# A float32r gather for two experts at a time, weights in runs of 8 KB, and one wait less in a mixture-of-experts layer

## The reference

```python
h2 = rms_norm(x, g_norm_ffn) * (1 + scale2) + shift2          # scale2, shift2: columns of c_act @ w_ada
p_group = softmax(h2 @ w_rg + b_rg);  g_sel = argmax            # 4 groups
logits_sel = (h2 @ w_re + b_re)[group g_sel]                    # 8 experts in the group
pi_top, e_in = top_k(softmax(logits_sel), 2)                    # 2 experts for each token
weights = pg_top * pi_top / sum(pi_top)
for e in range(32):                                             # the tokens that chose e
    h = silu(xc @ w_g[e]) * (xc @ w_u[e])                       # w_g, w_u: 1024 x 512
    y = (h @ w_d[e]) * weight                                   # w_d: 512 x 1024
x = x + gate2 * sum of a token's two y
```

## Time and profile before

| | |
|---|---|
| median of 3 runs | 1013.75 us |
| the profiled execution: its time | 1013.75 us |
| its span in the trace | 1011.9 us |
| TensorE (PE) busy | 924.4 us (91%) |
| VectorE (DVE) busy | 468.7 us (46%) |
| ScalarE (ACT) busy | 193.4 us (19%) |
| GpSimd (POOL) busy | 125.2 us (12%) |
| DMA | 271.01 MB, mean 268 GB/s |
| chain that ended last | DMA 41%, PE 41%, SP's queue 6%, DVE 5% |

### The profile page before, as it was taken

The page is one execution under the profiler, slowest core; times in us unless marked ns, Lnnn a source line. Parts: engine busy times, 40 slices in busy tenths (PEclk is TensorE's granted clock), DMA queues, the critical chain, the costliest instruction groups (busy, mean ns, idle before and its releaser), DMA issues.

```text
span 1011.9 us, 11514 instructions
## 1 busy us (share of the span) xinstructions
PE 924.4 (91%) x4335; PEld 497.7 (49%) x4335; DVE 468.7 (46%) x762; ACT 193.4 (19%) x327; POOL 125.2 (12%) x159
## 2 busy tenths in 40 slices
PE   3699999988989999699899999999999999999980
PEld 2266789977776665388433333333333333333330
DVE  2432555367687666523643343343343343343334
ACT  3432333333335332202100000000000000000000
POOL 1000222004223122600000000000000000000000
PEclk9799999998999999799999999999999999999996
DMA  9886672202050204623799999999999999999976
GB/s 347 289 284 229 220 245 84 84 1 95 22 156 27 84 1 166 248 100 124 281 380 396 392 397 393 395 395 394 397 393 396 392 397 393 395 395 396 396 277 257
DMA packets 116278, 271.01 MB, mean 268 GB/s; under 512 B 8565, under 2 KB 20869, under 8 KB 112661
## 3 DMA queue, kind: packets, MB, share of 16 engines
q1 hardware_dynamic: 112116, 264.41, 70.5%
q0 software_dynamic: 2944, 5.29, 1.5%
q10 hardware_dynamic: 1184, 0.87, 0.3%
HBM read 263.70 MB, written 11.03 MB: 272 GB/s over the span
## 4 chain that ended last, share of the span: by engine, by line
DMA 41%; PE 41%; SPq 6%; DVE 5%; issue 4%; ACT 3%; DVEq 0%; POOLq 0%; POOL 0%; ACTq 0%
DMA arena<-in_w_expert_up 38%; PE ps L639 23%; SPq L407 4%; PE ps L982 3%; PE ps L595 2%; PE ps L791 2%; SPq L362 2%; PE ps L1000 1%; PE ps L959 1%; PE ps L816 1%; DMA arena<-in_w_ada 1%; DMA arena<-y_rows 1%; ACT xn L1173 1%; PE ps L800 1%; PE ps L745 1%
## 5 line engine op out<-in xcount | busy, mean ns | idle before, releaser
L982 PE MATMUL ps<-arena,hT 128*64 128x512 f32 x1024 | 225.7, 592 | 3.5 <-DMA arena<-in_w_expert_up 1.9
L982 PEld LDWEIGHTS ps<-arena,hT 128*64 128x64 f32 x1024 | 73.7, 137 | 149.6 <-issue 145.1
L1000 PE MATMUL ps<-arena,hT 128*64 128x512 f32 x512 | 116.9, 598 | 0.6 <-issue 0.6
L959 PE MATMUL ps<-xn,hT 128*64 128x512 f32 x512 | 115.4, 592 | 0.9 <-DVE hT L1671 0.9
L639 PE MATMUL ps<-slot_r,xs_r 128*128 128x512 f32 x320 | 106.1, 404 | 0.5 <-issue 0.5
L639 PE MATMUL ps<-xs_r,slot_r 128*128 128x512 f32 x320 | 103.7, 406 | 3.0 <-DVE hT_r L1376 2.9
L1795 DVE TENSOR_SCALAR hT<-hT 128x256 f32<-128x256 f32 x32 | 9.4, 294 | 191.4 <-ACT hT L1282 191.4
L639 PE MATMUL ps<-slot_r,hT_r 128*128 128x512 f32 x224 | 88.6, 395 | 0.0
L639 PEld LDWEIGHTS ps<-slot_r,xs_r 128*128 128x128 f32 x320 | 77.1, 261 | 10.6 <-ACT arena L1147 2.5
L1282 ACT ACTIVATE hT<-ps 128x256 f32<-128x256 f32 x32 | 12.3, 384 | 359.2 <-PE ps L982 359.2
L959 PEld LDWEIGHTS ps<-xn,hT 128*64 128x64 f32 x512 | 36.6, 137 | 73.1 <-issue 72.0
(11 more groups left out here) (261 smaller groups left out, 963.5 us busy)
## 6 DMA issues: line engine op xcount, KB each, us to landing
arena<-in_w_expert_gate SPq DMA_DIRECT2D x64, 1024.0 KB, 13.2
arena<-in_w_expert_up SPq DMA_DIRECT2D x64, 1024.0 KB, 14.6
arena<-in_w_expert_down SPq DMA_DIRECT2D x32, 2048.0 KB, 17.0
xn<-in_w_ada SPq DMA_DIRECT2D x16, 1024.0 KB, 5.0
arena<-in_w_in SPq DMA_DIRECT2D x12, 1024.0 KB, 7.8
arena<-in_w_ada SPq DMA_DIRECT2D x8, 1024.0 KB, 14.3
arena<-in_w_branch_gate SPq DMA_DIRECT2D x4, 2048.0 KB, 8.4
xs<-in_x SPq DMA_DIRECT2D x8, 512.0 KB, 8.5
```

The lines of the kernel that those rows point to most:

```text
L959: mm = pe.matmul(ps[64 * h:64 * h + 64, 0, :], hot[:, hb, t, :], xn[:, t, h * CH:(h + 1) * CH], start=(t == 0), stop=(t == NT - 1), skip_g ...
L982: mm = pe.matmul(ps[64 * h:64 * h + 64, 2, :], xeT[:, k % 4, k // 4, :], w_gu(b)[:, :, k, 256 * h:256 * h + 256], start=(k == 0), stop=(k ...
L1000: mm = pe.matmul(ps[64 * h:64 * h + 64, 4, :], hhT[:, f % 2, 64 * (f // 2):64 * (f // 2) + 64], w_dn(b)[:, f, h * CH:(h + 1) * CH], start= ...
```

## The change

- Two experts are gathered with one 0/1 matrix of 128 slots (`hot_r`), in float32r. x1 is kept as two float32r parts, `xs_r` (rounded, by ScalarE) and `xn_r` (the rest, by GpSimd), and each part is multiplied, so a gather of one half of the width is 8 products of 128x512. It is no longer normalised before the gather: `rstd_by_slot` gathers 1/rms of each slot with four small products, VectorE adds the two parts (`keep_rstd`), and ScalarE applies it as it takes the gather from PSUM.
- Partition p holds rows 8p to 8p+7 of each weight (`by_run`), so all expert weights come in runs of 8 KB. x1, the router's weights, the gain and the two columns of scale and shift are laid out to match; the columns go through HBM (`columns` on GpSimd) and no longer through transposes.
- `refill` asks for both halves of gate and up at once.
- transpose_x stands ahead of transpose_h. One buffer of results (`ye`) takes the place of two. x1 as float32 is put together again by VectorE behind expert 30.

```diff
             def load_gu_half(e, b, kh):
-                rows = slice(kh * D // 2, (kh + 1) * D // 2)
...
-                    src = w[0, bass.ds(e, 1), rows].rearrange("e (k p) n -> p (e k) n", p=P)
-                    sp.dma_start(w_gu(b)[:, g, ks], src).then_inc(gu_in[b][kh], 16)
+                    src = w[0, bass.ds(e, 1)].rearrange("e (p k) n -> p (e k n)", k=KC)[:, run]
+                    sp.dma_start(w_gu(b)[:, g, ks].rearrange("p k n -> p (k n)"), src).then_inc(gu_in[b][kh], 16)
...
-            def refill(e, b, last, loads):
+            def refill(e, b):
                 sp.wait_ge(gu_ps, e + 1)
-                load_gu_half(e + NBUF, b, 0)
-                sp.wait_ge(gu_in[last][1], loads * 32)
-                load_gu_half(e + NBUF, b, 1)
+                load_gu(e + NBUF, b)
                 sp.wait_ge(dn_ps, e + 1)
                 load_dn(e + NBUF, b)
...
+            def columns(r):
+                at = 64 * (1 - r)
+                pool.wait_ge(mod_rows, r + 2)
+                pool.dma_start(mod_2[r].rearrange("(j n) -> j n", j=2), modr[at:at + 64:32, :]).then_inc(mod_out, 16)
+                pool.wait_ge(mod_out, 16 * (r + 1))
+                pool.dma_start(cols[:, 3 - r, :], by_run(mod_2[r])).then_inc(cols_in, 16)
...
+            for t in range(NT):
+                pool.wait_ge(hi1_ok, t + 1)
+                pool.wait_ge(x1t_ps, t + 1)
+                pool.tensor_tensor(xn_r[:, t, :], xn[:, t, :], xs_r[:, t, :].bitcast(F32), ALU.subtract
+                                   ).then_inc(lo1_ok, 1)
...
+            def rstd_by_slot(q):
...
                 for t in range(NT):
-                    for h in range(2):
-                        mm = pe.matmul(ps[64 * h:64 * h + 64, 0, :], hot[:, hb, t, :],
-                                       xn[:, t, h * CH:(h + 1) * CH], start=(t == 0), stop=(t == NT - 1),
-                                       skip_group_check=True)
+                    mm = pe.matmul(ps[:, 3, 256:258], hot_r[:, t, :], rstd_r[:, t, :], start=(t == 0),
+                                   stop=(t == NT - 1), skip_group_check=True)
+                mm.then_inc(sr_ps, 1)
+
+            def gather(g, half):
...
+                for t in range(NT):
+                    for part in (xs_r, xn_r):
+                        mm = pe.matmul(ps[:, 6 * half, :], hot_r[:, t, :], part[:, t, half * CH:(half + 1) * CH],
+                                       start=(t == 0 and part is xs_r), stop=(t == NT - 1 and part is xn_r))
...
-            def expert(e, b, hb, loads, more=True):
-                gate_up(e, b, loads)
+            def expert(e, b, loads, xb, j, pair, more=True):
+                gate_up(e, b, loads, xb, j)
                 if not later(e):
                     slot_tables(0)
                 if more:
-                    gather(e + 1, 1 - hb)
+                    if j == 0:
+                        rstd_by_slot(pair + 1)
+                    gather(e + 2, j)
+                    transpose_x(e + 2)
                 else:
                     keep_clock(3)
                 transpose_h(e)
-                if more:
-                    transpose_x(e + 1)
                 down(e, b, loads)
...
-                xt = xs[:, t, j * CH:(j + 1) * CH]
-                dve.tensor_tensor(xt, xt, out_ps, ALU.add).then_inc(x1_ok, 1)
+                xt = xs[:, t, j * CH:(j + 1) * CH].rearrange("p (c k) -> p k c", k=KC)
+                dve.tensor_tensor(xn[:, t, :].rearrange("p (k c) -> p k c", k=KC)[:, :, 64 * j:64 * j + 64], xt,
+                                  out_ps.rearrange("p (c k) -> p k c", k=KC), ALU.add).then_inc(x1_ok, 1)
...
+            for e in range(NE - 4, NE):
+                expert(e, e % 2, e // 2, e // 2 % 2, more=(e < NE - 2))
+                if e == NE - 2:
+                    for t in range(NT):
+                        link(dve.tensor_tensor(x1n[:, t, :].rearrange("p (c k) -> p c k", k=KC),
+                                               xs_r[:, t, :].bitcast(F32).rearrange("p (k c) -> p c k", k=KC),
+                                               xn_r[:, t, :].bitcast(F32).rearrange("p (k c) -> p c k", k=KC),
+                                               ALU.add))
```

More of the change, by code:

```diff
@@ L224, in hybrid_layer @@
                                     for i in range(3))
-        idx = [sb(f"idx{b}", [P, 1], I32) for b in range(2)]
+        idx = sb("idx", [P, 1], I32)
+        rstd_r = sb("rstd_r", [P, NT, 2], F32R)
+        slot_rstd = sb("slot_rstd", [P, 1])
+        x1n = arena[:, EXP_W:EXP_W + NT * D].rearrange("p (t n) -> p t n", t=NT)
         wcol = sb("wcol", [P, 1])
@@ L569, in store @@
                 pool.indirect_dma_start(
[L570 to L578, removed]
+                    out=y_rows, out_offset=bass.IndirectOffsetOnAxis(ap=idx[:, 0:1], axis=0),
+                    in_=ye, in_offset=None, bounds_check=last_row, oob_is_err=False,
+                ).then_inc(y_out, 16)
+            store(0, 0)
+            with pool.Fori(1, NE) as e:
+                store(e, e)
             def pool_round(rnd):
@@ L936, in keep_clock @@
                 for _ in range(n):
[L937 removed]
+                    pe.matmul(ps[:, 5, 0:SEQ], ident[:], gate2h, start=True, stop=True)
             keep_clock(6)
@@ L970, in transpose_x, with gate_up @@
                 mm.then_inc(xt_ps, 1)
-            def gate_up(e, b, loads):
+            def gate_up(e, b, loads, xb, j):
                 pe.wait_ge(gu_in[b][0], loads * 32)
-                pe.wait_ge(xt_ok, e + 1)
+                pe.wait_ge(xt_ok, (e - j) + 1)
                 if later(e):
@@ L1842, in dve_round @@
                 assert at[0] == ROUND_STEPS
-                with dve.Fori(0, NE) as e:
+                with dve.Fori(0, NE // 2) as i:
                     dve.wait_ge(tables_ok, rnd + 1)
-                    k = rnd * NE + e
-                    one_hot(e, 0, k)
-                    xm, b2 = store_xT(k)
-                    store_xT2(k, xm, b2, k * NSTEP + 1)
-                    expert(k, 0, rnd * NE + (e - NE // 2), more=False, col=e)
+                    q = rnd * (NE // 2) + i
+                    one_hot(i, q)
+                    keep_rstd(q)
+                    for j in range(2):
+                        store_xT(q * 2 + j, j, 0)
+                    for j in range(2):
+                        expert(q * 2 + j, j, q, 0, more=False, col=i * 2 + j)
             ROUND_STEPS = 3 + 4 * NT
```

357 lines of the change are left out of this document (192 added, 165 removed).

## The result

The changed kernel takes 1021.0 us (median of 5 runs, 1018.81 to 1024.64) against 1013.54 in the same series: a ratio of 1.0069, 95% interval 1.0050 to 1.0088. It is slower by 0.7%. I had forecast 1015.0 and a range of 1009 to 1020, so the measured time lies 1 us outside the range. Its profiled execution took 1021.0, the span is 1019.2 us, 7.3 more than before.

What follows compares the result with a forecast made beforehand. TensorE's order of work was taken to set the pace, with DMA 2 us behind at the end. The terms, 1013.75 - 2.2 + 2.4 - 0.9 + 0.3 + 0.35 + 1.6 = 1015.3, gave a forecast of 1015, range 1009 to 1020.

Steps and rivals of the forecast that it cites:

- 31 periods at full clock: From down of expert 0 to down of expert 31: 472.3 us against 474.49, so -2.2 (-5 to +2).
- start, work alone: Before expert 0's down: two gathers ahead of the first gate_up and a later one-hot, +2.4 us (+1 to +4).
- columns: Before the experts: two sets of four transposes leave the chain where TensorE is the bound, -0.9 us (-1.5 to 0).
- router and x1's addition: Before the experts: GpSimd's subtraction delays VectorE and so the router, +0.3 us; the strided last x1 addition grows by +0.35.
- expert 30's additions: Four strided VectorE additions ahead of expert 31's silu, 1.92 us each at 1.64 times the length: +1.6 (0 to +4).
- DMA term: Expert weight loads in 8 KB runs flow at 422 GB/s, which gains the 2.05 us of late loads and no more.
- Two of the signs: Expected in the expert loop if the forecast is right: L1029 waiting for VectorE, and DMA below full share.
- rival D: Expert loads: the new row distance slows HBM below 395 GB/s; at 370 it costs +35 us, 1049; chance 0.04.
- rival F: Expert loads: without the wait, gate and up requests crowd out down; judged none, the queue's order staying the same.
- Rival A: Strided additions cost nothing (-1.95 us) and even experts pay less than 0.2 (-3.5): 1009 to 1012; chance 0.27.
- Rival C: VectorE's additions behind expert 30 hold up expert 31 from 1.55 us each; at 2.5 they cost 4; 1017 to 1021; chance 0.20.
- rival E: New gaps on TensorE let its granted clock fall from 2.4 to 1.2 GHz: 1018 to 1030 us; chance 0.06.

Runs made afterwards that it cites:

- experiment 10: Changed kernel with closing additions split behind experts 29 and 30, plus idle products in TensorE's gaps at the start: 1012.8 us, ratio 0.9978 to the kernel before.
- experiment 1: Changed kernel with the four closing additions moved from behind expert 30 to behind expert 31: 1018.89 us, ratio 1.0034 to the kernel before.
- experiment 5: Changed kernel with the removed wait for a landing put back between the halves of gate and up: 1020.67 us, ratio 1.0054 to the kernel before.
- experiment 8: Changed kernel with nine instead of three idle products beside expert 31's silu: 1020.21 us, ratio 1.0050 to the kernel before.
- experiment 6: Kernel before with expert weights loaded in runs of 8 KB and nothing else changed (output off): 1010.2 us, ratio 0.9966 to the kernel before.
- experiment 3: Changed kernel with the closing additions read in order and written in steps of 8 numbers: 1016.86 us, ratio 1.0022 to the kernel before.
- experiment 2: Changed kernel with all three operands of the closing additions contiguous, still behind expert 30: 1015.33 us, ratio 1.0007 to the kernel before.
- experiment 9: Changed kernel with two of the strided closing additions behind expert 29 and two behind expert 30: 1015.29 us, ratio 0.9998 to the kernel before.
- experiment 7: Changed kernel with expert weights loaded in the old runs of 2 and 4 KB (output off): 1022.03 us, ratio 1.0067 to the kernel before.
- experiment 12: Changed kernel without the four 128x2 products and their sum for pairs 1 to 15: 1013.33 us, ratio 0.9984 to the kernel before.
- experiment 4: Changed kernel with idle products in TensorE's gaps around the early gathers at the start: 1019.4 us, ratio 1.0047 to the kernel before.
- experiment 11: Changed kernel with split additions behind experts 29 and 30, read in order and written in steps, plus idle start products: 1012.9 us, ratio 0.9985 to the kernel before.

## Why the prediction was wrong, point by point

| term | predicted | measured | from |
|---|---|---|---|
| 31 periods at full clock | -2.2 | -2.4 | 985.17 - 513.13 = 472.04 in experiment 10; 474.42 before |
| start, work alone | +2.4 | +2.0 | 513.13 - 490.77 = 22.4 in experiment 10 against 20.6, and 0.26 for the wider one-hot |
| start, clock | 0 | +4.0 in this execution, +1.4 in others | L985 to the end of expert 0's down: 30.0 in the change, 26.0 in experiment 10; 27.4 in experiments 1, 5 and 8 |
| columns | -0.9 | not told apart | see below |
| router and x1's addition | +0.65 | +0.7 | L1704 to L1724: 487.88 - 473.38 = 14.5; before 488.94 - 475.14 = 13.8 |
| expert 30's additions | +1.6 | +3.1 | gate_up to down: 990.17 - 975.60 = 14.57; 985.17 - 973.74 = 11.43 in experiment 10 |
| last down, clock | 0 | +1.7 | 5.37 against 3.67 |

Together 9.1 us with the +4.0; less 1.8 us by which the last x1 was reached earlier, that is the 7.3 us between the two spans.

**The experts.** Right in sum and in both parts. I had 15.04 and 15.47, they are 15.10 and 15.38. The DMA term holds too, by experiment 6 (-2.3 against -2.05; I had counted 15.24 for the last period, which takes 15.03 without a gather), and so does its limit: the expert loads flow at 420 to 423 GB/s in the page's slices (415 in the window of 700 to 960), and no more than the waits of experts 30 and 31 can be had. Two of the signs I named were off. L1029 doesn't wait for VectorE in the steady state, since the four transposes of L1007 end at 711.91, just as the silu is ready (its last step ends at 711.85 in the timeline). And the DMA engines stay at a full share (1.00). The row distance of 16 KB costs nothing that shows (rival D falls: it needed less than 395 GB/s), and the wait that was removed was nothing (experiment 5, rival F as I had it). Rival A's sum names 15 even experts; there are 14, and its -3.5 is for 14.

**The closing additions: the step that failed by size.** I took a ratio of 1.64 from a weight load, a read on another engine, because it was the nearest row. The addition reads two operands in steps of 128 numbers and took 2.39 us against 1.24 in the earlier trace rows, 1.93 times as long. Rival C had the rest of the mechanism right: by its sum (1.25 + 4 x 2.43 - 7.5) additions of 2.39 us cost 3.5 (measured 3.1), and those of 2.0 in experiment 3 cost 1.9 (measured 1.8), so the point of 1.55 us from which they decide fits, though no run stands at it. Experiments 2 and 9 take the delay away in two different ways and give the same time. The Trainium skill ("SBUF — State Buffer", the note on cachelines) warns of such reads and has no size; the trace agrees with the warning and gives the size.

**The clock: the step that was missing.** I put the clock at nothing in the sum, and gave rival E 0.06, by the steady state: TensorE busy for 13.6 of 15 us. There the granted clock did stay at 1.00. But I had listed new gaps myself, at the start (each step there now waits for another engine) and at the end (silu late), and did not ask for the clock in these two places. My ground, that the page shows falls only where TensorE had waited for long, was read from slices of 25 us. The trace of before has a fall just ahead of the experts that these slices hide, after an idle time of 0.78 us between short products:

```profile
478.50 1.97 PE L898 MATMUL ps<-wr,arena 128*128 128x36 f32 x16 [0.78 <-DVE arena L1633]
```

```profile
480.00:483.00 3.00, 3.00 (x9) 1.59 (x9) 2.18 (x10) 3.00 (x4) 0.00 (x0) 0.62 1.01 368
```

At the start of the change the gaps of 1.2 and 1.3 us were followed by 0.50 to 0.55, which cost 4.0 us in the trace. The two falls aren't equally sure. The first, worth 1.4 us, stands in the traces of all nine kernels without idle products in the gaps (the change and experiments 1 to 3, 5, 7 to 9 and 12), and in none of the three with them (4, 10, 11). The second, worth 2.6, stands in five of the eight that also keep the step for even experts, and is absent in experiments 1, 5 and 8, whose code and gaps at the start are those of the change. What decides between them is not shown. So idle products take away the first fall; for the second three traces with them don't suffice. At the end TensorE was idle for 3.88 us ahead of L1029, and the last down ran 1.7 us longer; nothing of that is left where the gap is smaller (0.73 us in experiments 2 and 9, 2.42 in 3) or filled (experiment 8), and it is there in each of the four traces with the full delay (the change, 4, 5 and 12). So C and E came together, and one set off a part of the other. Experiments 9 and 10 take both out, 8.2 us by the medians and 9.2 by the ratios.

**The router.** As predicted in sum. GpSimd's last subtraction lies beside the router's second step:

```profile
479.81 1.42 DVE small L1754
```

```profile
478.71 2.35 POOL L585 TENSOR_TENSOR xn_r<-xn,xs_r 128x1024 fp32r<-128x1024 f32 x1 [4.08 <-ACT xs_r L1315]
```

It took 0.31 in the earlier trace rows, so it came 1.1 us late where I had 1.5. The strided addition for the last x1 (L1708) took 1.10 against 0.69 (the length of L1655 in the trace of before, and not half of the earlier trace rows, as I had written), 1.59 times as long. It was the case that my 1.64 fitted.

**The columns.** Open. The two places in the trace of after, and the first of them before:

```profile
473.38 0.71 DVE ps L1704
474.12 1.10 DVE xn L1708
...
487.88 0.70 DVE hT_r L1724
```

```profile
475.14 0.70 DVE L1651 TENSOR_TENSOR ps<-ps,xn 128x512 f32<-128x512 f32 x1 [2.04 <-PE ps L639]
```

The last x1 is reached at 473.38 instead of 475.14, 1.8 us earlier where I had 0.9. But in experiment 6, with all its column transposes, the same place is also 2.0 us early (L1633 at 475.76, before 477.75). And the twelve kernels whose code up to there is that of the change reach it anywhere from 470.7 (experiment 11) to 476.7 us (experiment 5), 473.6 in the mean. One execution of each can't give this term. No run took the columns alone.

## What to carry to other kernels

Where a stage's engines hand work to each other with gaps of a microsecond, ask for the granted clock of that stage in windows of a few microseconds, not of the steady state and not in slices of 25, and price each new gap at the work behind it at half the clock. A fall can come in one execution and not in the next, so look at more than one trace before giving it a price. Work that is put "where VectorE is free" has a room with an end: count how much fits before the next expert's step, and put the rest one period earlier, before trying to make it shorter. A resource that seems to hold 38% of the chain was worth 2.3 us; the distance between its pace and the next engine's over the whole stretch, less the lead of the buffers, is what it can give.

## What the runs showed of the hardware that I had not expected

- A VectorE addition of 128x1024 float32 from SBUF took 1.22 to 1.24 us with everything contiguous, 1.95 to 2.04 with a write in steps of 8 numbers, and 2.21 to 2.50 with two reads in steps of 128 numbers. With one such operand in PSUM and one in SBUF, both read in steps of 8, one of 128x512 took 1.10 instead of 0.69.
- Beside VectorE's additions of two SBUF operands GpSimd's smallest work and its scatter took longer: 2.02 instead of 0.19 us, and 4.04 instead of 2.64 (experiment 1). In the other direction a VectorE step of 0.31 us took 1.42 beside a GpSimd subtraction.
- After an idle gap of 1.2 us between short products the granted clock went down to 1.2 GHz in nine traces of nine, and after one of 1.3 us in five of eight. With idle products in the gaps (one of 128x512 in each, one of 128x256 behind each early gather) it stayed at 2.4 in three of three. The kernel before fell to 1.2 GHz in its router, after 0.78 us, but not after its gaps of 0.94 and 1.67 us from 489 us on, between longer float32 products. After a gap of 3.9 us at the end the clock fell for the last down, and after one of 2.61 us inside gate_up for the half behind it (experiment 7); after one of 2.42 us in experiment 3 it did not.
- Four products of 128x128 by 128x2 took 0.54 to 0.61 us, over a quarter of the 1.96 us of eight products of 128x512.
